# A transformer stack on one core: an eighteenth home for experts' weights, side work placed one unit later, and the first input loaded in smaller pieces

## The chip, the cores and the metric

The kernel runs on one core of one Trainium2 chip. The metric is device time in microseconds (us). Several executions are timed, and their median is compared. TensorE (PE) multiplies, VectorE (DVE) and ScalarE (ACT) do elementwise work, GpSimd (POOL) does little here, and SyncE (SP) issues nearly all DMA transfers.

## What is computed

256 tokens of width 1024 pass through a first block of two layers and then a second block of two layers. Cut to what matters for this change:

```python
def first_block(x, ...):                    # two layers
    for i in range(2):
        mix = (gla_mixer, mlstm_mixer)[i](h, ...)
        h = layer_norm(ALPHA * h + mix, ...)
        ffn = grouped_moe(h, router_w, moe_w1[i], moe_w3[i], moe_w2[i])
        h = layer_norm(ALPHA * h + ffn, ...)

def grouped_moe(t, ...):                    # 16 experts, each token uses 2
    for e in range(16):
        h = silu(t @ w1[e]) * (t @ w3[e])   # 1024 x 512 each
        y = y + gates[:, e] * (h @ w2[e])   # 512 x 1024

def second_block(x, ...):                   # two layers of two attentions and an MLP
    for l in range(2):
        parts = rms(x) modulated @ w_in     # q, k with rms and rotation, v, gates
        x = x + gt1 * ((gate_a * y_a + gate_b * y_b) @ w_out)
        x = x + gt2 * (relu(h2 @ w_ff1) ** 2 @ w_ff2)
```

All operands are float32. All of the weights are read once from HBM, 420 MB in all.

## The kernel before, in words

**Chunks, halves and units.** The weights come as chunks of 128 x 2048 floats, 1 MB each, in the order of use (`build`, L3235). A chunk has two halves, and a half is a unit of PE work. For most products a half is split: ACT copies it rounded into `hi` (L1661) and DVE subtracts into `lo` (L2111), and PE multiplies hi and lo apart. There are five pairs of hi and lo buffers. The experts' chunks are used raw, without a split. Between the weights lie chunks named `ada`, which DVE alone uses: it adds each one, scaled, to a sum (`ada_step`, 2.3 us apiece).

**Homes.** A chunk lies in a home of 8 KB per partition. Six homes `raw0` to `raw5` are always there. While an experts' stage runs, buffers that it doesn't need are homes too: `ACC`, pieces of the big scratch `AR`, and the five `ring` homes, which lie over the hi and lo buffers. `spare` (L3255) lists triples (home, first, last): the home is opened for the chunk `first` of the stage and may be used again up to `last`. `places` (L145) gives each chunk its home: the one opened for it, or the open one used longest ago. An experts' stage has 96 chunks and 17 homes in turn before the change.

**The load queue.** SP goes through the chunks in order (`load`, L2978). Before a transfer it waits until the home's last chunk is used up, and, where a home is opened, for what else used that memory: the ring homes wait for the last unit before the stage (`ring_free`, L750), ACC for `sum_up`, the home `ar2048` in the first stage for `x` (0, 1), which is DVE's last ln_x step. A chunk whose home isn't free holds up all that follow.

**The order of the work.** One generator per stage (`walk_gla` L256, `walk_moe` L303, `walk_mlstm` L390, `walk_attention` L511) yields jobs in one order, and each of the five engines runs through the same generator and does its own share of each job. So a job's place in the generator is its place in the queue of every engine. Between the units of a projection stands side work (`Side.advance`), so many jobs after each unit.

- In an experts' stage `p` counts pairs of experts (0 to 7) and `s` the steps of four units (3.65 us of PE each). A `gather` of PE, DVE and ACT writes the tokens of four experts, in four parts `gather g, 0..3`, into half `g % 2` of XG, which is the buffer `TF` (the same memory as `T2`, whose halves are TH and TL elsewhere). Group 1 is read from p = 2 on; its parts stand at p = 0 (s = 2 and 3) and p = 1 (s = 1 and 4).
- In the mLSTM mixer, `pace` (L450) says how much side work follows each unit of `og`: 0, 1, 2, then 3. `scores 3` follows the second unit, and `values` (0, 0) and (1, 0) the third. On DVE `scores 3` is the weighting of the scores. `values` on PE waits for it.
- In the attentions, `rope n` is a chain of DVE jobs on segment n of q and k (its last is `rope_add`, L2823), and `qk_turn n` (L1491) the transposes of its result on PE, which come LAG = 2 units later (`turns`, L520).

**The start.** The input xT (1 MB, as eight blocks k) comes in two transfers into F with the first half chunk between them, in the order SP L3022 to L3030: x 0, first half, x 1, second half of chunk 0, `vec`, chunk 1, `cst`, chunk 2, `wgu` (34 KB). ACT and DVE split x in four `xs` jobs and the weights in `hi` and `lo`. PE does unit 0, then `glr` (needs all of x, and vec), unit 1, then `z` (needs wgu), and then the next units.

## Time and profile before

| | us |
|---|---|
| three timed runs | 1482.96, 1483.88, 1484.76 |
| median | 1483.88 |
| the profiled execution, its own time | 1485.66 |
| its span in the trace | 1483.8 |
| PE busy | 1443.6 |
| DVE busy | 910.2 |
| ACT busy | 626.7 |
| bytes moved | 420.17 MB |

The profile is of one execution. Its span is 1.9 us shorter than its own time, which holds what lies before the first and after the last instruction. A row of a timeline gives start, duration, engine, line, operation, output and inputs, and in brackets the idle time of the engine just before and what ended it. "issue" there means that the profile shows nothing that the engine waited for. Matmuls overlap, so their durations add up to more than the time between their starts.

### The profile page before, as it was taken

The page shows a single profiled execution, that of the slowest core. Times are in us where ns is not written, and L with a number is a line of the kernel's source. Part 1 is how long each engine was busy: PE and PEld are TensorE (multiplying, and loading weights), DVE is VectorE, ACT ScalarE, POOL GpSimd, SP SyncE. Part 2 cuts the span into 40 slices and gives each one's busy share as a digit, 9 for nine tenths or more (in the row PEclk, how much of TensorE's full clock was granted, in tenths as well). Part 3 has the DMA queues.
Part 4 walks back from the last instruction along what each step waited for, and adds up shares of the span by engine and source line. Part 5 has one row for each costly group of instructions (what it writes and reads, how often), then busy time and mean ns, then how long its engine had stood idle before and what let it go on. Part 6 is the DMA issues. An engine that isn't in the chain of part 4 may idle for free.

```text
span 1483.8 us, 20474 instructions
## 1 busy us (share of the span) xinstructions
PE 1443.6 (97%) x8383; PEld 1068.5 (72%) x8383; DVE 910.2 (61%) x1549; ACT 626.7 (42%) x1004; POOL 40.8 (3%) x39
## 2 busy tenths in 40 slices
PE   9999999989999999999799999999999999999998
PEld 7885444436888544443578897999988898799997
DVE  4986111118787611111799888997968976775555
ACT  6453211115334321211555655454456566465443
POOL 0000000000000000000210000000002000000000
PEclk9999999999999999999899999999999999999999
DMA  9897999998467899999665463899955533445540
GB/s 379 314 365 301 426 427 426 427 426 329 166 247 297 331 424 427 427 426 426 247 231 184 181 232 142 335 369 352 357 182 187 197 123 125 151 170 193 179 168 29
DMA packets 59062, 420.17 MB, mean 283 GB/s; under 512 B 6657, under 2 KB 6721, under 8 KB 8658
## 3 DMA queue, kind: packets, MB, share of 16 engines
q1 hardware_dynamic: 58322, 417.17, 71.5%
q0 software_dynamic: 640, 1.61, 0.4%
q8 instruction: 69, 1.13, 0.3%
q14 instruction: 31, 0.25, 0.0%
HBM read 417.71 MB, written 1.05 MB: 282 GB/s over the span
## 4 chain that ended last, share of the span: by engine, by line
PE 80%; DVE 11%; DMA 4%; ACT 3%; issue 1%; SPq 0%; DVEq 0%; ACTq 0%
PE ps L869 78%; DVE lo L2111 2%; DMA AR<-in_moe 2%; DMA raw<-in_moe 2%; DVE AR L2104 2%; PE ps L1520 1%; DMA AR<-in_wgu 1%; DVE AR L2101 1%; PE ps L1491 1%; ACT AR L2011 1%; PE ps L1244 1%; DVE TINY L2104 1%; DVE ACC L2104 0%; PE ps L991 0%; PE ps L1001 0%
## 5 line engine op out<-in xcount | busy, mean ns | idle before, releaser
L2111 DVE TENSOR_TENSOR lo<-raw,hi 128x1024 fp32r<-128x1024 f32 x296 | 359.4, 1237 | 97.7 <-ACT hi L1661 97.0
L1661 ACT ACTIVATE hi<-raw 128x1024 fp32r<-128x1024 f32 x296 | 306.2, 1056 | 183.3 <-PE ps L869 178.1
L869 PE MATMUL ps<-T,hi 128*128 128x256 f32 x1792 | 323.8, 283 | 1.4 <-DVE lo L2111 0.6
L869 PE MATMUL ps<-hi,T 128*128 128x512 f32 x896 | 285.8, 396 | 1.0 <-DVE lo L2111 0.6
L869 PEld LDWEIGHTS ps<-T,hi 128*128 128x128 f32 x1792 | 277.1, 189 | 10.0 <-issue 5.1
L869 PE MATMUL ps<-T,lo 128*128 128x256 f32 x896 | 249.2, 280 | 0.0
L869 PEld LDWEIGHTS ps<-hi,T 128*128 128x128 f32 x896 | 169.0, 189 | 38.0 <-DVE lo L2111 2.1
L869 PE MATMUL ps<-lo,T 128*128 128x512 f32 x448 | 172.8, 390 | 0.0
L869 PEld LDWEIGHTS ps<-T,lo 128*128 128x128 f32 x896 | 169.2, 189 | 0.3 <-DVE lo L2111 0.3
L869 PE MATMUL ps<-hi,AF 128*128 128x512 f32 x512 | 163.3, 391 | 0.0
L2104 DVE SCALAR_TENSOR_TENSOR AR<-AR,ps 128x512 f32<-128x512 f32 x52 | 35.4, 684 | 192.0 <-PE ps L869 104.8
L869 PE MATMUL ps<-raw,TF 128*64 128x512 f32 x424 | 128.2, 595 | 3.0 <-issue 3.0
L869 PE MATMUL ps<-AR 128*64 128x512 f32 (+7 forms) x612 | 108.6, 408 | 4.7 <-POOL AR L2907 1.3
L869 PEld LDWEIGHTS ps<-hi,AF 128*128 128x128 f32 x512 | 96.2, 188 | 19.5
L869 PE MATMUL ps<-AR,TF 128*64 128x512 f32 x328 | 107.7, 595 | 0.5 <-DMA AR<-in_moe 0.5
L1857 ACT ACTIVATE AF<-ps,TINY 128x512 fp32r<-128x512 f32 x32 | 22.0, 688 | 195.5 <-PE ps L869 195.5
L2104 DVE SCALAR_TENSOR_TENSOR AF<-ps,TINY,AF 128x512 fp32r<-128x512 f32 x32 | 24.0, 750 | 124.6 <-ACT AF L1857 124.6
L869 PE MATMUL ps<-lo,AF 128*128 128x512 f32 x256 | 99.9, 390 | 0.0
L869 PEld LDWEIGHTS ps<-lo,T 128*128 128x128 f32 x448 | 84.5, 189 | 16.8
L869 PEld LDWEIGHTS ps<-raw,TF 128*64 128x64 f32 x424 | 39.5, 137 | 63.2 <-issue 62.4
L869 PEld LDWEIGHTS ps<-AR 128*64 128x64 f32 (+2 forms) x612 | 58.8, 163 | 33.6 <-issue 20.8
L2104 DVE SCALAR_TENSOR_TENSOR ACC<-raw,TINY,ACC 128x2048 f32<-128x2048 f32 x28 | 65.6, 2344 | 0.2
(247 smaller groups left out, 1730.5 us busy)
## 6 DMA issues: line engine op xcount, KB each, us to landing
raw<-in_moe SPq DMA_DIRECT2D x76, 1024.0 KB, 17.1
raw<-in_b_ff SPq DMA_DIRECT2D x64, 1024.0 KB, 5.3
AR<-in_moe SPq DMA_DIRECT2D x59, 1024.0 KB, 17.1
raw<-in_ada SPq DMA_DIRECT2D x48, 1024.0 KB, 6.7
ring<-in_moe SPq DMA_DIRECT2D x45, 1024.0 KB, 15.8
raw<-in_b_in SPq DMA_DIRECT2D x24, 1024.0 KB, 6.0
raw<-in_b_gate SPq DMA_DIRECT2D x16, 1024.0 KB, 4.8
ACC<-in_moe SPq DMA_DIRECT2D x12, 1024.0 KB, 20.2
```

Source lines behind the costliest of these rows:

```text
L869: return e.matmul(o, l, r, start=a, stop=z, skip_group_check=True)
L1244: ins = e.transpose(p[:, 128 * f:128 * f + 128], m.GR[:, 128 * f:128 * f + 128], ident)
L1491: ins = e.transpose(p[:, 256 * x + 128 * q:256 * x + 128 * q + 128], m.RT[n % 2][:, q, 128 * (p0 + x):128 * (p0 + x) + 128], ident)
L1520: ins = e.transpose(p[:, 256 * k + 128 * q:256 * k + 128 * q + 128], m.PB[j % 8][:, q, 128 * k:128 * k + 128], ident)
L1661: e.activation(hi[n % NC][:, :], raw[place[c]][:, 1024 * half:1024 * half + 1024], ACT.Copy).then_inc(*to("hi", "hi", n))
L1857: e.activation(m.YH[:, HALF[n]], PS[bank["down", i, x, n]][:, :], ACT.Copy, scale=m.GS[:, x:x + 1]).then_inc(*to("tile_out", "y_hi", i, x, n))
L2011: ins = e.activation(o, src, ACT.Exp, scale=m.SC, bias=mx[:, q:q + 1], accum_out=sm[:, 2 + 2 * k + q:3 + 2 * k + q])
L2101: return e.tensor_scalar(o, a, s1, s2, op0=op0, op1=op1)
L2104: return e.scalar_tensor_tensor(out=o, in0=a, scalar=s, in1=b, op0=op0, op1=op1)
L2111: tt(lo[n % NC][:, :], r, hi[n % NC][:, :], SUB).then_inc(*to("lo", "lo", n))
```

## The change

It has four parts, in the order in which they act:

1. The input: xT comes in four transfers of 256 KB instead of two of 512 KB, and the first half chunk in two of 256 KB, in the order x 0, w 0, x 1, w 1, x 2, x 3. The split of that half chunk and its products are divided the same way (`hi_first`, `lo_first`, and a job `rest` for the second part), and unit 0 waits piece by piece.
2. The second half of TF becomes home 13, for chunk 11 of each experts' stage alone; it opens with `ring_free`. Ring, ACC and (in the first stage) ar2048 open one, one and two chunks later. That half of TF is XG's group 1, so the four gathers of group 1 move behind chunk 11's use: two at p = 1, s = 2 and two at p = 1, s = 4.
3. In the mLSTM mixer the pace becomes 0, 0, 3, 3, ...: `scores 3` moves behind the third unit of `og` and stands directly before the two `values` there.
4. In both attentions `qk_turn 0` comes one unit later.

```diff
--- before.py
+++ after.py
@@ -256,8 +256,10 @@
 def walk_gla(feed):
     for g in range(4):
         yield ("xs", g)
+        if g == 0:
+            yield from feed.ahead(1)
         if g == 1:
-            yield from feed.ahead(1)
+            yield ("rest",)
 
     def prepare():
         yield [("glr",), ("constants",)]
@@ -359,9 +361,9 @@
         if 0 < p < 8 and s == 4:
             yield ("turn", p)
         if p < 6:
-            for k, at in enumerate((1, 4) if p else (2, 3)):
+            for k, at in enumerate((2, 2, 4, 4) if p == 1 else (1, 4) if p else ()):
                 if s == at:
-                    yield ("gather", p // 2 + 1, 2 * (p % 2) + k)
+                    yield ("gather", p // 2 + 1, k if p == 1 else 2 * (p % 2) + k)
 
     for p in range(9):
         for s in range(6):
@@ -447,7 +449,7 @@
         yield ("turn", 0)
         yield ("turn", 1)
 
-    pace = iter((0, 1, 2) + 13 * (3,))
+    pace = iter((0, 0) + 14 * (3,))
     yield from run_b("og", 2, 8, feed, lambda: side.advance(next(pace)), end=gate_first)
     route = routing()
     rows = iter([[("ln_x", t, s)] for t in range(2) for s in range(2)] + 4 * [[]])
@@ -517,7 +519,7 @@
         yield [("rope_norm", n)]
         for q in range(len(SEGS[n][0])):
             yield [("rope_turn", n, q)]
-        turns.append([LAG, n])
+        turns.append([LAG + (n == 0), n])
         pending.append(n)
         yield [("rope_add", n)]
 
@@ -713,7 +715,7 @@
         chunks, stops = small["chunks"], small["stops"]
         place, before, turn, uses = places(chunks, [s for i in range(2) for s in small["spare"][i]])
         raw += [ACC, ar(4096, 2048), ar(6144, 2048), ar(11264, 2048), ar(13312, 2048), ar(15360, 2048), ar(2048, 2048)]
-        raw += [x[:, :] for x in ring] + [ar(0, 2048)]
+        raw += [x[:, :] for x in ring] + [ar(0, 2048), TF[:, 2048:4096]]
         ACCS = [ACC[:, :], ar(11264, 2048), ar(13312, 2048)]
         plan = Feed(chunks, ())
         while plan.at < len(plan.events):
@@ -723,7 +725,7 @@
         def loaded(c, half=1):
 
             if c == 0 and half == 0:
-                return after("head")
+                return after("head", 1)
             return signal(f"raw{place[c]}"), 16 * turn[c]
 
         def emptied(c):
@@ -902,14 +904,16 @@
                 if u == 0:
 
                     n0 = plan.units[u][2]
-                    w.wait_ge(*after("hi", n0))
                     for ks in (range(4), range(4, 8)):
-                        for k in ks:
-                            if k % 2 == 0:
-                                w.wait_ge(*after(*xs[k // 2]))
-                            mm(o, hi[n0][:, 128 * k:128 * k + 128], th[:, k, :], k == 0, False)
-                            mm(o, hi[n0][:, 128 * k:128 * k + 128], tl[:, k, :], False, False)
-                        w.wait_ge(*after("lo", n0))
+                        w.wait_ge(*after("hi", n0) if ks[0] else after("hi_first"))
+                        for k in (ks[0], ks[2]):
+                            w.wait_ge(*after("xs_hi", k // 2))
+                            for j in (k, k + 1):
+                                mm(o, hi[n0][:, 128 * j:128 * j + 128], th[:, j, :], j == 0, False)
+                            w.wait_ge(*after(*xs[k // 2]))
+                            for j in (k, k + 1):
+                                mm(o, hi[n0][:, 128 * j:128 * j + 128], tl[:, j, :], False, False)
+                        w.wait_ge(*after("lo", n0) if ks[0] else after("lo_first"))
                         for k in ks:
                             ins = mm(o, lo[n0][:, 128 * k:128 * k + 128], th[:, k, :], False, k == kt - 1)
                 else:
@@ -1077,8 +1081,8 @@
                     elif what == "glr":
                         p = take("glr")
                         glr = VE["glr"].rearrange("p (k r) -> p k r", k=8)
-                        w.wait_ge(*after("x_t", 0))
-                        w.wait_ge(*after("x_t", 1))
+                        for g in range(4):
+                            w.wait_ge(*after("x_t", g))
                         w.wait_ge(*after("vec"))
                         for k in range(8):
                             ins = mm(p[0:16, 0:256], glr[:, k, :], F[:, k, :], k == 0, k == 7)
@@ -1651,6 +1655,10 @@
 
                 u = plan.splits[n]
                 c, half, _ = plan.units[u]
+                if n == 0:
+                    w.wait_ge(*after("head", 0))
+                    e.activation(hi[0][:, HALF[0]], raw[place[c]][:, HALF[0]], ACT.Copy).then_inc(*to("hi", "hi_first"))
+                    return
                 w.wait_ge(*loaded(c, half))
                 if n >= NC:
                     w.wait_ge(*after("used", plan.splits[n - NC]))
@@ -1722,8 +1730,11 @@
                         hi_part(a[0])
                     elif what == "xs":
                         two = slice(2 * a[0], 2 * a[0] + 2)
-                        w.wait_ge(*after("x_t", a[0] // 2))
+                        w.wait_ge(*after("x_t", a[0]))
                         e.activation(TH[:, two, :], F[:, two, :], ACT.Copy).then_inc(*to("column", "xs_hi", a[0]))
+                    elif what == "rest":
+                        w.wait_ge(*loaded(0, 0))
+                        e.activation(hi[0][:, HALF[1]], raw[place[0]][:, HALF[1]], ACT.Copy).then_inc(*to("hi", "hi", 0))
                     elif what == "glr":
                         w.wait_ge(*after("glr"))
                         w.wait_ge(*after("gl_one"))
@@ -2106,6 +2117,10 @@
             def lo_part(n):
 
                 c, half, _ = plan.units[plan.splits[n]]
+                if n == 0:
+                    w.wait_ge(*after("hi_first"))
+                    tt(lo[0][:, HALF[0]], raw[place[c]][:, HALF[0]], hi[0][:, HALF[0]], SUB).then_inc(*to("lo", "lo_first"))
+                    return
                 w.wait_ge(*after("hi", n))
                 r = raw[place[c]][:, 1024 * half:1024 * half + 1024]
                 tt(lo[n % NC][:, :], r, hi[n % NC][:, :], SUB).then_inc(*to("lo", "lo", n))
@@ -2331,6 +2346,9 @@
                         two = slice(2 * a[0], 2 * a[0] + 2)
                         w.wait_ge(*after("xs_hi", a[0]))
                         tt(TL[:, two, :], F[:, two, :], TH[:, two, :], SUB).then_inc(*to("v_split", "xs", a[0]))
+                    elif what == "rest":
+                        w.wait_ge(*after("hi", 0))
+                        tt(lo[0][:, HALF[1]], raw[place[0]][:, HALF[1]], hi[0][:, HALF[1]], SUB).then_inc(*to("lo", "lo", 0))
                     elif what == "constants":
                         u, g0 = tiny("c_u", 8), small["vec"][0]["gla_g"][0]
                         w.wait_ge(*after("c_tanh"))
@@ -2971,7 +2989,7 @@
 
         def sync_program(e):
             w = Waits(e)
-            xT = D["xT"].rearrange("p (g k i) -> p g k i", g=2, k=4)
+            xT = D["xT"].rearrange("p (g k i) -> p g k i", g=4, k=2)
             opens = {first: (i, p) for i in range(2) for p, first, _ in small["spare"][i]}
             first_of = {c0 - 12: i for c0, i in stops.items()}
 
@@ -2985,7 +3003,7 @@
                     i, q = opens[c]
                     if q == 0:
                         w.wait_ge(*after("sum_up", (0, i)))
-                    elif 6 < q < 12:
+                    elif 6 < q < 12 or q == 13:
                         w.wait_ge(*after(*ring_free(i)))
                     elif i == 0:
                         if q > 5:
@@ -3019,9 +3037,10 @@
                     at["f_load", i, x] = (signal(f"full_raw{i}"), 96 * (x + 1))
                 v.wait_ge(*after("f_done", i))
 
-            e.dma_start(F[:, 0:4, :], xT[:, 0]).then_inc(*landed("x_t", 0))
-            e.dma_start(raw[0][:, 0:1024], chunks[0][1][:, 0:1024]).then_inc(*landed("head"))
-            e.dma_start(F[:, 4:8, :], xT[:, 1]).then_inc(*landed("x_t", 1))
+            for g in range(4):
+                e.dma_start(F[:, 2 * g:2 * g + 2, :], xT[:, g]).then_inc(*landed("x_t", g))
+                if g < 2:
+                    e.dma_start(raw[0][:, HALF[g]], chunks[0][1][:, HALF[g]]).then_inc(*landed("head", g))
             load(0, 1024)
             e.dma_start(vec[:, :], D["vec"]).then_inc(*landed("vec"))
             load(1)
@@ -3249,10 +3268,10 @@
             i, at = int(n[3]), len(chunks) - count
             moe[i] = chunks[at:]
             stops[len(chunks)] = i
-            early = (((4, 0, 95), (5, 1, 76), (3, 5, 5), (1, 6, 95), (2, 7, 95), (6, 19, 95)) if i == 0 else
+            early = (((4, 0, 95), (5, 1, 76), (3, 5, 5), (1, 6, 95), (2, 7, 95), (6, 21, 95)) if i == 0 else
                      ((12, -2, 95), (6, -1, 95), (1, 5, 95), (2, 7, 95), (5, 10, 76)))
-            ring = tuple((7 + n, 11 + n, 80) for n in range(5))
-            spare[i] = [(p, at + c, at + last) for p, c, last in (*early, *ring, (0, 16, 95))]
+            ring = ((13, 11, 11), *((7 + n, 12 + n, 80) for n in range(5)))
+            spare[i] = [(p, at + c, at + last) for p, c, last in (*early, *ring, (0, 17, 95))]
     small = {"cst": (cst_at, D["cst"].shape[1]), "vec": (vec_at, D["vec"].shape[1]), "chunks": chunks, "stops": stops, "moe": moe,
              "moe_at": [c - len(moe[i]) for c, i in stops.items()], "spare": spare}
     return two_block_kernel(nc, aps, out, small)
```

## Rows read from the trace of the kernel before

**Rows 1.** The page's part 4: share of the chain that ended last, by engine.
```profile
PE 80%; DVE 11%; DMA 4%; ACT 3%; issue 1%; SPq 0%; DVEq 0%; ACTq 0%
```

**Rows 2.** Windows in the two experts' stages: busy us of each engine, PEclk, DMA share, GB/s.
```profile
134.00:136.00 2.00, 2.00 (x18) 1.42 (x14) 0.34 (x1) 0.00 (x0) 0.00 (x0) 1.00 0.48 147
141.00:144.00 3.00, 2.38 (x12) 0.73 (x9) 2.79 (x13) 0.00 (x0) 0.00 (x0) 1.00 0.58 167
508.00:511.00 3.00, 3.00 (x20) 1.90 (x20) 1.52 (x3) 0.00 (x0) 0.00 (x0) 1.00 0.72 213
250.00:300.00 50.00, 50.00 (x242) 19.99 (x240) 6.38 (x12) 7.74 (x14) 0.00 (x0) 1.00 1.01 426
```

**Rows 3.** Timeline of PE, end of the first experts' stage.
```profile
304.68 3.65 PE L869 MATMUL ps<-AR,TF 128*64 128x512 f32 x16 [0.47 <-DMA AR<-in_moe]
...
319.71 0.61 PE L869 MATMUL ps<-AR 128*64 128x512 f32 x1 [0.48 <-DMA raw<-in_moe]
...
324.57 3.65 PE L869 MATMUL ps<-raw,AR 128*64 128x512 f32 x16 [0.61 <-DMA raw<-in_moe]
329.39 0.61 PE L869 MATMUL ps<-ACC,AR 128*64 128x512 f32 x1 [1.17 <-issue]
```

**Rows 4.** Timeline of SP's queue, start of the first experts' stage.
```profile
118.16 2.28 SPq L3005 DMA_DIRECT2D ring<-in_moe  x5
...
134.52 7.28 SPq L3005 DMA_DIRECT2D AR<-in_moe  x3
```

**Rows 5.** Timeline of PE at p = 0, s = 2 of the first experts' stage.
```profile
143.70 0.39 PE L869 MATMUL ps<-FR,AF 128*128 128x256 f32 x1 [0.62 <-DVE FR L2455]
```

**Rows 6.** Timeline of PE, end of the second experts' stage.
```profile
696.69 3.65 PE L869 MATMUL ps<-AR 128*64 128x512 f32 x16 [0.43 <-DMA AR<-in_moe]
...
701.52 0.61 PE L869 MATMUL ps<-ACC,AR 128*64 128x512 f32 x1 [1.18 <-issue]
```

**Rows 7.** Timeline of PE and DVE in the mLSTM mixer's `og`.
```profile
440.47 3.49 DVE L2111 TENSOR_TENSOR lo<-raw,hi 128x1024 fp32r<-128x1024 f32 x3
440.69 1.55 PE L869 MATMUL ps<-AR 128*128 128x256 f32 x8 [1.29 <-DVE AR L2104]
...
443.87 0.55 DVE L2104 SCALAR_TENSOR_TENSOR AR<-ps,AR 128x384 f32<-128x384 f32 x1
...
444.34 2.34 DVE L2104 SCALAR_TENSOR_TENSOR ACC<-raw,TINY,ACC 128x2048 f32<-128x2048 f32 x1
...
444.85 0.50 PE L869 MATMUL ps<-cst,AR 128*128 128x1 f32 x4
...
446.60 2.35 DVE L2111 TENSOR_TENSOR lo<-raw,hi 128x1024 fp32r<-128x1024 f32 x2
```

**Rows 8.** Timeline of PE and DVE in the first attention: `qk_turn 0`, `rope_add 1`, `qk_turn 1`.
```profile
756.89 1.97 PE L1491 MATMUL ps<-cst,AR 128*128 128x128 f32 x8 [2.65 <-DVE AR L2823]
...
767.29 0.96 DVE L2823 TENSOR_TENSOR AR<-AR 128x768 f32<-128x768 f32 x1
...
770.14 0.82 PE L1491 MATMUL ps<-cst,AR 128*128 128x128 f32 x6
```

**Rows 9.** Timeline of PE and DVE in the second attention, the same three.
```profile
1136.34 1.10 PE L1491 MATMUL ps<-cst,AR 128*128 128x128 f32 x8 [1.08 <-DVE AR L2823]
...
1146.73 0.96 DVE L2823 TENSOR_TENSOR AR<-AR 128x768 f32<-128x768 f32 x1
...
1148.20 0.82 PE L1491 MATMUL ps<-cst,AR 128*128 128x128 f32 x6
```

**Rows 10.** Window after the wait of Rows 8, columns as in Rows 2.
```profile
756.00:760.00 4.00, 3.11 (x12) 2.87 (x13) 3.97 (x4) 1.20 (x2) 0.00 (x0) 0.57 0.24 47
```

**Rows 11.** Timeline of PE at the start: `glr` and `z`.
```profile
11.09 3.63 PE L869 MATMUL ps<-F,vec 128*16 128x256 f32 x16
...
18.30 1.95 PE L869 MATMUL ps<-AR 17*128 17x512 f32 x4 [0.51 <-DMA AR<-in_wgu]
```

**Rows 12.** DMA issues: tensors, queue, count, KB each, median us from issue to landing.
```profile
F<-in_xT SPq DMA_DIRECT2D x2, 512.0 KB, 5.3
out_dram<-X SPq DMA_DIRECT2D x4, 256.0 KB, 2.0
```

## The prediction

> **What bounds the kernel now.** I read the chain that ended last first: PE holds 80% of it, DMA 4%, DVE 11% [rows 1]. So a change pays only where PE stands still, and I looked for those places with PE's timeline, and for their cause with windows and with SP's queue. In the experts' stages the DMA runs at 426 GB/s with a share of 1.01 while PE is busy too [rows 2]; PE uses chunks faster than they come, lives on what the homes held at its start, and runs dry near the end: 0.47 + 0.48 + 0.61 + 1.17 = 2.73 us in the first stage [rows 3] and 0.43 + 1.18 = 1.61 us in the second [rows 6]. The two waits marked "issue" stand before the step that reads ACC, in the run of DMA waits, so I count them as DMA. Elsewhere PE waits for DVE: 1.29 us in og [rows 7], 2.65 and 1.08 us at `qk_turn 0` [rows 8, 9].
>
> Of the profiled execution's 1485.66 us, 1483.8 are span; it lies 1.78 us above the median of 1483.88. I sum against it and take the difference over to the median. About 0.2% (3.0 us) is what a measurement of this kernel can tell from no change.
>
> **The experts' stages (part 2).** In a stage that the DMA ends, only idle time of the DMA after it has begun can be won. The five ring loads are issued at 118.16, the next ones that wait for PE at 134.52, three of them over 7.28 us [rows 4]. In between and after, the DMA falls to 147 GB/s for 2 us and to 167 GB/s for 3 us [rows 2]. Against 426 GB/s that is 2 x 279/426 = 1.31 and 3 x 259/426 = 1.82, together 3.13 us. The extra chunk takes 1.05 MB / 426 GB/s = 2.46 us and is issued with the ring, so it covers the first gap and pushes the rest of the queue back. The second gap is the third load of 134.52, which waited for DVE's last ln_x (the home ar2048) and held the loads behind it; it now stands two chunks later, behind a load whose home is free at about the end of s = 1. I take both gaps as closed: -3.13 us. PE can use that much: its DMA waits are 2.73 us, and 0.62 us of waiting for `one_hot 1` goes as the gather moves away [rows 5], in all 3.35. **First stage: -3.1 us.** In the second stage there is one gap, 213 GB/s over 3 us [rows 2], 3 x 213/426 = 1.50 us, and the waits of 1.61 can take it. **Second stage: -1.5 us.** Bounds for the pair: 0 (the idle time only moves) and -3.35 - 2.23 = -5.6, all of PE's waits with 0.62 in each. The gathers are the same count; they move from p = 0 to p = 1 and end at the same s = 4, a step before p = 2 reads them, and PE has the slack of the waits at the end. SP issues no more transfers here, only another address.
>
> **The mLSTM pace (part 3).** The wait of 1.29 us before `scores 3` goes: the third unit starts at 440.69 - 1.29 = 439.40, and the unit and the scores, which took 444.85 - 440.69 = 4.16 us [rows 7], are done at 443.56. But now the job's place on DVE has moved too. Between the old place and the new one DVE's order holds an ada step and a lo. Before, DVE did three lo, the weighting (443.87), ada (444.34), lo (446.60) [rows 7], and was never idle. After, it does three lo until 443.87, ada for 446.60 - 444.34 = 2.26, lo for 2.35 / 2 = 1.18 and only then the weighting, 0.55: done at 447.86. `values` (0, 0) needs it and now stands right behind the scores, so PE starts it at about 447.9 where it started at 444.85: **+3.05 us**, a wait of 4.3 us in place of one of 1.29. The units and values after it shift as a whole; the next lo are early enough.
>
> Such a wait has a second price. After the wait of 2.65 us [rows 8] the granted clock was 0.57 of full over the next 4 us, that is mostly at 1.2 instead of 2.4 GHz [rows 10], and the same jobs from `qk_turn 0` to `qk_turn 1` took 770.14 - 756.89 = 13.25 us there and 1148.20 - 1136.34 = 11.86 us behind the wait of 1.08 [rows 8, 9]. I charge that 1.39 once: **+1.4**. Part 3: +4.45; bounds -1.3 (no new wait) and +5.85 (two such stretches).
>
> **`qk_turn 0` a unit later (part 4).** In the first attention PE is free at 756.89 - 2.65 = 754.24. It does a unit first, and the result of `rope_add 0` is then there. The wait goes, and so does the slow stretch: after 11.86 us of the same jobs PE stands at `qk_turn 1` at 766.10. `rope_add 1` ends at 767.29 + 0.96 = 768.25, in a chain in which DVE has no gap, so it won't come sooner: a new wait of 2.15 us. `qk_turn 1` starts at 768.3 for 770.14: **-1.84**. Whether 2.15 us of waiting lowers the clock lies between the wait of 1.08 [rows 9], behind which the same jobs ran faster, and that of 2.65; half of 1.39: **+0.7**. Second attention: at `qk_turn 1` by 1136.34 - 1.08 + 11.86 = 1147.12, `rope_add 1` done at 1147.69, start 1147.75 for 1148.20: **-0.45**. Behind that, DVE's next waits are on PE and shift along. Bounds: -4.04 - 1.08 = -5.1 (no new wait) and 0.
>
> **The input (part 1).** Smaller pieces let unit 0 begin and end sooner, by an estimated 1 us (half of 512 KB at 426 GB/s is 0.6 us, and the copies behind it are half as long). Then `glr`, which started at 11.09 without a wait, can come forward, but `z` waits 0.51 us for wgu at 18.30 already [rows 11], and wgu stands behind the same bytes in the same queue. What is won ahead of it becomes a longer wait there, some 1.5 us: **0**. SP issues three transfers more, 2.28 / 5 = 0.46 us each [rows 4], so wgu's issue comes 1.4 us later; the bytes queued ahead of wgu hide that, and without them it would cost those 1.4. Bounds: -0.5 (the wait that is there) and +4.2 (below).
>
> The Trainium skill speaks against this part: DMA: Bandwidth & Descriptors, section Measured (HBM→SBUF, 128 partitions, SWDGE, issued from GpSimd), asks for transfers of at least 1 MiB, and its fit, 2.0 us plus the bytes over 436 GB/s for each, would put three transfers more at 6 us if they ran one after another, an estimate from that page; the sum would then be +4.3 in place of -1.7.
>
> **Sum.** -3.1 - 1.5 + 3.05 + 1.4 - 1.84 + 0.7 - 0.45 + 0 = -1.74: 1485.66 becomes 1483.9, and the median of 1483.88 becomes **1482.1 us**, within what counts as no change, on its fast side.
>
> **Rivals.** (a) *The weighting doesn't end up late.* If DVE comes to it before the ada step's end, or the shift is made up behind it (PE waits again before the heads' transposes, so the chain there isn't all PE), part 3 gives between -1.3 and 0: 1476.4 to 1477.7, taken as 1477. For it: the new wait is worked out from DVE's order alone, and no row shows it. Against: DVE works without a break through that stretch [rows 7]. Chance 0.25, always faster.
> (b) *The extra home does nothing.* The idle time of the DMA moves to a later place, because some other home is late in its turn, and the end of the stage stays: -4.6 goes, 1486.7. Against: in the middle of the stage the DMA has a share of 1.01 [rows 2]. It decides if the DMA's share falls anywhere between the ring loads and the stage's end. Chance 0.10, half of it beyond 0.2% on the slow side.
> (c) *The small transfers pay one by one*, the rival on the slower side. A transfer of 256 KB took 2.0 us alone [rows 12], where its bytes at 426 GB/s need 0.62: 1.4 us more for each. Three more in a row ahead of wgu are +4.2, and a wait at `z` of that length brings the 1.4 of the clock: 1482.1 + 5.6 = 1487.7. It decides from the point where the pieces no longer overlap; against it, a piece of 512 KB lands 5.3 us after its issue [rows 12] while the next ones were issued within 0.5 us, so they overlap now. Chance 0.07. The rule of the page above is this rival.
> (d) *The granted clock takes more*: a second slow stretch in og and one in the first attention, +2.1: 1484.2, still no change; it is held by the forecast's range.
>
> **How the numbers follow.** Forecast with (d): 0.55, own range 1479 to 1485; 0.15 of it lies under 1480.9 and 0.03 above 1486.9. (a) 0.25, (b) 0.10, (c) 0.07, 0.03 for what I don't see. Faster: 0.15 + 0.25 = 0.40. Slower: 0.03 + 0.05 + 0.07 = 0.15. Same: 0.45. The range takes in most of (a) and half of (b): 1475.8 to 1487.0.
>
> **What would show it.** Right: no window under 400 GB/s from the ring loads to the end of either experts' stage, PE's DMA waits there under 1 us; PE waiting some 4 us for a DVE L2104 ahead of `values` with the granted clock under 1 behind it; no wait at `qk_turn 0` and about 2 us at `qk_turn 1` of the first attention; `z` still starting at about 18.3. Wrong: `z` much earlier or later, a PE without a wait in og, or gaps of the DMA in a new place.

## The result and the profile after

The changed kernel took **1488.38 us** (median of 9 runs, 1486.43 to 1489.34) beside 1484.76 us for the kernel before on the same chip (9 runs, 1482.96 to 1486.76). The ratio is 1.0021, with a 95% interval from 1.0012 to 1.0029: slower by 3.6 us, just over what a measurement of this kernel can tell. The forecast was 1482.1 us and no change, with a range up to 1487.0: wrong, in the sign too. Four executions, three of the kernel before and one of a run below, took 2330 us and more; they are left out of every ratio.

The profiled execution of the changed kernel took 1486.71 us at a mean granted clock of 0.994; the nine runs have 0.992 in the mean. (1 - clock) times the span is about the time given up to the clock: 8.9 us in the profiled execution and 11.2 in the mean. So the profile shows the change with 2.3 us less of the slow clock than it usually has.

Windows of the kernel after, columns as in [rows 2]:

```profile
134.00:136.00 2.00, 2.00 (x14) 1.09 (x10) 0.00 (x0) 0.00 (x0) 0.00 (x0) 1.00 1.05 434
141.00:144.00 3.00, 3.00 (x18) 1.00 (x16) 2.79 (x12) 0.00 (x0) 0.00 (x0) 1.00 1.02 431
144.00:146.00 2.00, 2.00 (x12) 0.71 (x10) 0.89 (x2) 0.00 (x0) 0.00 (x0) 1.00 0.97 365
508.00:511.00 3.00, 3.00 (x22) 1.99 (x22) 1.00 (x2) 1.78 (x4) 0.00 (x0) 1.00 1.03 431
446.00:450.00 4.00, 3.65 (x16) 3.32 (x16) 1.34 (x2) 0.00 (x0) 0.00 (x0) 0.61 1.01 426
450.00:454.00 4.00, 4.00 (x12) 3.25 (x12) 0.00 (x0) 0.00 (x0) 0.00 (x0) 0.54 1.02 432
```

The gaps of the DMA of [rows 2] are closed (434 for 147, 431 for 167 and 213 GB/s; 365 in one window is all that is left of them). The last two rows are new: in og PE works at a granted clock of 0.61 and 0.54, that is mostly at 1.2 GHz instead of 2.4, for 6.8 us.

Timeline of the kernel after, PE and DVE, at the places of [rows 3, 7, 8, 11]; the row at 458.73 is where DVE takes over from PE's last `values`, and the one at 469.31 the first step of PE behind the norm of the mLSTM mixer:

```profile
11.56 3.63 PE L871 MATMUL ps<-F,vec 128*16 128x256 f32 x16
18.91 1.95 PE L871 MATMUL ps<-AR 17*128 17x512 f32 x4 [0.66 <-DMA AR<-in_wgu]
...
322.84 3.65 PE L871 MATMUL ps<-raw,AR 128*64 128x512 f32 x16 [0.38 <-DMA raw<-in_moe]
327.68 0.61 PE L871 MATMUL ps<-ACC,AR 128*64 128x512 f32 x1 [1.19 <-issue]
...
442.26 2.35 DVE L2115 SCALAR_TENSOR_TENSOR ACC<-raw,TINY,ACC 128x2048 f32<-128x2048 f32 x1
444.52 1.22 DVE L2126 TENSOR_TENSOR lo<-raw,hi 128x1024 fp32r<-128x1024 f32 x1
445.65 0.55 DVE L2115 SCALAR_TENSOR_TENSOR AR<-ps,AR 128x384 f32<-128x384 f32 x1
446.35 0.58 PE L871 MATMUL ps<-cst,AR 128*128 128x1 f32 x4 [4.54 <-DVE AR L2115]
...
458.73 0.17 DVE L2678 COPY TINY<-ps 128x8 f32<-128x8 f32 x1 [11.39 <-PE ps L871]
...
469.31 1.06 PE L995 MATMUL ps<-cst,AR 128*128 128x128 f32 x8 [0.57 <-DVE AR L2115]
...
761.09 1.09 PE L1495 MATMUL ps<-cst,AR 128*128 128x128 f32 x8
772.50 0.87 PE L1495 MATMUL ps<-cst,AR 128*128 128x128 f32 x6 [2.13 <-DVE AR L2841]
```

The same two rows in the kernel before:

```profile
453.84 0.17 DVE L2660 COPY TINY<-ps 128x8 f32<-128x8 f32 x1 [4.89 <-PE ps L869]
464.42 1.06 PE L991 MATMUL ps<-cst,AR 128*128 128x128 f32 x8 [0.57 <-DVE AR L2104]
```

Read as differences to the rows before, these give the balance of the profile. `z` is 0.61 later (18.30). The two steps with a wait at the end of the first experts' stage come 1.73 and 1.71 earlier (324.57 and 329.39). The step behind the mixer's norm is 4.89 later, so the mixer lost 6.60. From the start of `values` to that point it takes 12.38 us for 8.99 (458.73 - 446.35, 453.84 - 444.85), and from there through DVE and ACT to the step behind the norm 10.58 us in both. `qk_turn 1` of the first attention is 2.36 later (770.14), so 2.53 came back in the second experts' stage and the attention. The span ends 1.1 later.

The kernel's other lines hardly moved: PE holds 80% of the chain that ended last and DVE 12%, for 80% and 11% in [rows 1].

### The profile page after: what moved, and what is told of

The parts are those of the page before. It is cut to its first block, busy times and chain, and to the rows that moved or that the text cites. A ratio compares the mean times of both kernels' runs of the same rounds, so it can differ in the third digit from the quotient of the medians.

```text
span 1484.9 us, 20479 instructions
## 1 busy us (share of the span) xinstructions
PE 1443.7 (97%) x8383; PEld 1068.7 (72%) x8383; DVE 911.3 (61%) x1550; ACT 626.1 (42%) x1005; POOL 39.3 (3%) x39
## 3 DMA queue, kind: packets, MB, share of 16 engines
q8 instruction: 69, 1.13, 0.3%
HBM read 417.71 MB, written 1.05 MB: 282 GB/s over the span
## 4 chain that ended last, share of the span: by engine, by line
PE 80%; DVE 12%; DMA 4%; ACT 3%; issue 1%; SPq 0%; DVEq 0%; ACTq 0%
PE ps L871 77%; DVE lo L2126 3%; DVE AR L2115 2%; DMA AR<-in_moe 1%; DMA raw<-in_moe 1%; PE ps L1524 1%; DMA AR<-in_wgu 1%; DVE ACC L2115 1%; DVE AR L2112 1%; DVE TINY L2115 1%; PE ps L1248 1%; ACT AR L2022 1%; PE ps L995 0%; PE ps L1495 0%; DVE TINY L2112 0%
## 5 line engine op out<-in xcount | busy, mean ns | idle before, releaser
L871 PE MATMUL ps<-raw,TF 128*64 128x512 f32 x432 | 135.0, 595 | 1.4 <-issue 1.4
L871 PE MATMUL ps<-AR 128*64 128x512 f32 (+7 forms) x636 | 126.2, 421 | 3.2 <-POOL AR L2925 1.3
L871 PEld LDWEIGHTS ps<-AR 128*64 128x64 f32 (+2 forms) x636 | 64.9, 165 | 38.5 <-issue 26.7
```

The costliest lines, as they stand in the source:

```text
L871: return e.matmul(o, l, r, start=a, stop=z, skip_group_check=True)
```

## The experiments

All were timed in turns with the kernel before (median 1484.6 to 1485.3 us in the four groups); differences are those of the medians, each to the kernel before of its own group.

**The parts taken apart.** First the change without part 3:

```diff
-    pace = iter((0, 0) + 14 * (3,))
+    pace = iter((0, 1, 2) + 13 * (3,))
```

> The changed kernel with the pace of og put back to 0, 1, 2, 3, ... (parts 1, 2 and 4 stay). Theory A (the weighting late on DVE costs its wait of 3.2 us and then two stretches of PE at half clock, together 6.5 us from og to the next norm, and nothing gives it back): 1488.4 - 6.5 = 1481.9, that is 2.9 under the kernel before; no granted clock under 1 in og. Theory B (the prediction's size, one slow stretch, 4.45 us): 1483.9. Theory C (what DVE loses in og is made up behind it, and the slower time comes from elsewhere): over 1486.5.

Measured: 1481.59 us, ratio 0.9972 (0.9960 to 0.9984), 3.75 less than before; no granted clock under 1 in og. Theory A. Part 3 alone turns a gain into the loss: 1488.4 - 1481.6 = 6.8 us by the medians, 3.6 + 3.75 = 7.4 when each is set against the kernel before that was timed beside it.

The change without part 1 (its hunks of the diff undone):

> The changed kernel with the input loaded as before (parts 2, 3 and 4 stay). Theory A (the split input makes z 0.61 us later, since wgu is issued 2.2 us later, and all that follows shifts by it, the opening of the ring homes too): 0.6 us less, 1487.8, z at 18.3. Theory B (the experts' stage that follows is ended by the DMA and swallows the 0.6): 1488.4, with z at 18.3 all the same. Theory C (the four small transfers help and z was late by chance): over 1488.6.

Measured: 1488.23 us, ratio 1.0018 (1.0010 to 1.0027) where the change has 1.0021; `z` at 18.80 in its profile, where A and B had 18.3. The intervals overlap: this run can't tell A from B. Only that part 1 is not the cause follows.

The kernel before with part 2 alone:

> The kernel before with the eighteenth home alone (part 2: the home, the gathers, the shifted openings). Theory A (the DMA's gap goes, but the last chunks land out of step, as read in the trace of the changed kernel, so PE gets 2.3 us of the first stage and 0.7 of the second): 3.0 less than before. Theory B (the prediction's size, 3.1 and 1.5): 4.6 less. Theory C (the home does nothing by itself, the gain came from other parts): under 1 less.

Measured: 1481.54 us, ratio 0.9974 (0.9965 to 0.9982), **3.8 less**, between A and B. In its profile the last ACT step of the first stage comes 2.13 sooner (338.71 to 336.58), and from there to the end of the second stage another 0.77 (372.14 to 371.37 us): 2.9 of the 3.8, as theory A has it. The rest has no place in the trace; the runs of the two kernels spread by 5 us each.

The kernel before with part 3 alone:

```diff
-    pace = iter((0, 1, 2) + 13 * (3,))
+    pace = iter((0, 0) + 14 * (3,))
```

> The kernel before with the pace 0, 0, 3, 3, ... alone (part 3). Theory A: 6.5 us more than before, with a wait of about 4.4 us ahead of values (0, 0) and two stretches of PE at half clock behind it. Theory B (the prediction's size): 4.45 more, one stretch. Theory C (only in the changed kernel, where the stage starts at another time, is the wait there): under 1.5 more.

Measured: 1493.13 us, ratio 1.0054 (1.0041 to 1.0067), **7.8 more**, over both. Windows of this run behind the wait, columns as before, and its two steps of PE:

```profile
444.00:448.00 4.00, 0.14 (x2) 0.00 (x0) 4.00 (x4) 0.00 (x0) 0.00 (x0) 1.00 0.65 244
448.00:452.00 4.00, 3.32 (x13) 2.99 (x13) 1.67 (x3) 0.00 (x0) 0.00 (x0) 0.60 1.01 424
452.00:456.00 4.00, 4.00 (x13) 3.37 (x14) 0.00 (x0) 0.00 (x0) 0.00 (x0) 0.50 1.01 426
456.00:460.00 4.00, 4.00 (x13) 3.17 (x12) 0.00 (x0) 0.60 (x1) 0.00 (x0) 0.62 1.02 430
```

```profile
448.68 0.89 PE L869 MATMUL ps<-cst,AR 128*128 128x1 f32 x4 [4.54 <-DVE AR L2104]
...
473.25 1.06 PE L991 MATMUL ps<-cst,AR 128*128 128x128 f32 x8 [0.58 <-DVE AR L2104]
```

The wait is the same 4.54 us to the hundredth. What differs is the clock: 10.2 us at half here (0.60, 0.50 and 0.62 in the rows), 6.8 in the changed kernel's profile. The change without part 1 has the same wait of 4.54 us too, and 10.2 us at half, of which 1.6 lie in the wait itself; its two steps are 23.85 us apart (446.23 and 470.08).

**What part 3 costs, in two terms.** To tell the late weighting from the clock, PE was given products of constants to do in the wait. They go into the bank that `values` is about to overwrite, so nothing else changes:

```diff
                         p = take("values1", t, hp)
+                        if t == hp == 0:
+                            for _ in range(10):
+                                mm(p[:, 0:256], C["tri3"][:, 0:128], C["tri3"][:, 0:256], True, True)
```

A first try had 17 products and misjudged their price:

> The kernel before with the pace 0, 0, 3, 3, ... (as in the run that took 7.8 us more), and 17 matmuls of constants on PE (128x256, 0.245 us each by the rows of values, 4.2 us in all) in the wait ahead of values (0, 0); their result is overwritten. The weighting on DVE is as late as before, so the wait itself stays paid. Theory A (of the 7.8 us the late weighting is 3.1 to 3.7, the rest the half clock behind the idle stretch): the granted clock stays 1.00 in og and the time is 3.1 to 3.7 more than before. Theory B (the clock has no part; the late values hold up DVE's chain to the next norm by more than their own delay): still 7 to 8 more, whatever the clock. Theory C (the clock falls for the kind of work behind, not for the idle stretch): clock 0.5 behind the fill all the same, and 7 to 8 more.

Measured: 1491.66 us, 7.1 more than before. Each product shows as two matmuls in the trace, and the fill took 7.50 us instead of 4.2, so `values` itself came 2.6 us later still (it starts 111.90 us behind the last ACT step of the experts' stage, for 109.28 in the run before this and 106.14 in the kernel before). The clock stayed at 1.00. Undecided, but the price was now known, and 10 products fit:

> Part 3 alone with 10 products of constants in the wait ahead of values (0, 0), 0.44 us each as the first fill showed, 4.4 us for a wait of 4.5. Theory A (the loss of 7.8 is 3.1 of late weighting and 4.7 of half clock behind the idle stretch): values (0, 0) starts 3.1 to 3.3 later than in the kernel before, og's norm by the same, granted clock 1.00, time 3.0 to 4.0 more than before. Theory B (the loss lies behind the late values and not in the clock): 7 to 8 more.

Measured: 1488.18 us, ratio 1.0020 (1.0011 to 1.0028), **3.0 more**. Timeline and windows of this run:

```profile
443.12 4.48 PE L869 MATMUL ps<-cst 128*128 128x256 f32 x20
447.12 0.55 DVE L2107 SCALAR_TENSOR_TENSOR AR<-ps,AR 128x384 f32<-128x384 f32 x1
447.73 0.61 PE L869 MATMUL ps<-cst,AR 128*128 128x1 f32 x4
...
467.38 1.06 PE L991 MATMUL ps<-cst,AR 128*128 128x128 f32 x8 [0.56 <-DVE AR L2107]
```

```profile
443.00:447.00 4.00, 4.00 (x21) 3.54 (x20) 4.00 (x3) 0.07 (x1) 0.00 (x0) 1.00 0.64 217
447.00:451.00 4.00, 3.87 (x24) 3.25 (x23) 1.81 (x3) 0.00 (x0) 0.00 (x0) 1.00 1.02 426
```

The weighting is as late as before and `values` waits for it as long, but PE isn't idle, and the clock stays at 1.00. Theory A: of the 7.8 us 3.0 are the late weighting and 4.8 the clock, the one good to 1.3 us and the other to about 2 by the intervals. The clocks of the runs agree: in the mean they are 0.9916 with the idle wait and 0.9951 with the filled one, as in the kernel before beside it (0.9951); 0.0035 of the span is 5.2 us. The Trainium skill says it in TensorE: Matmul & The Clock Gate, section Part 1: The HAM clock gate (the "warmup" mystery): "the default state is throttled, and activity releases the throttle". This trace agrees, with 0.50 behind 4.54 us of idling and 1.00 behind the same time filled.

**Where units can't cover.** If `values` only lacks the weighting, a unit of PE ahead of it should hide the wait. Two paces on parts 2 and 4 (which alone run at 3.6 under before, below):

```diff
-    pace = iter((0, 1, 2) + 13 * (3,))
+    pace = iter((0, 0, 1, 2) + 12 * (3,))   # the second run: (0, 0, 1, 0) + 12 * (3,)
```

> Parts 2 and 4 with the pace 0, 0, 1, 2, 3, ...: scores 3 behind the third unit as in the change, but the two values behind the fourth. Theory A (PE runs in order, so what the weighting lacks is covered by one unit of 2.85): the wait ahead of values is 4.5 - 2.85 = 1.7 in place of 4.5, the wait of 1.29 is gone, the clock stays up after so short a wait: +0.4 against parts 2 and 4 with the old pace, no change that can be measured. Theory B (any wait over 1.5 there lowers the clock): +2 to +4. Theory C (the late weighting was not the cause of the loss, but scores 3 behind the third unit): +6.5.

> Parts 2 and 4 with the pace 0, 0, 1, 0, 3, ...: scores 3 behind the third unit, values behind the fifth, so that two units of 2.85 stand between them. Theory A (the only harm was the wait for the weighting): no wait of PE for the weighting at all, -1.3 against parts 2 and 4 with the old pace. Theory B (the later values make the norm behind og late, which is then waited for): 0 to +2. Theory C (scores 3 behind the third unit is the harm): +6.5.

Measured: 1488.72 us (ratio 1.0019, 1.0008 to 1.0030) and 1485.81 us (1.0011, 1.0002 to 1.0020), that is 7.0 and 4.1 more than parts 2 and 4. My theory A fell in both. By size none holds: the first run fits C's 6.5, but the second contradicts C, and both passed B. In kind it is B, as the profiles show. Timeline of PE, the steps `values` (0, 0) and the one behind the norm, first run and second:

```profile
445.17 0.58 PE L869 MATMUL ps<-cst,AR 128*128 128x1 f32 x4 [1.78 <-DVE AR L2104]
...
468.10 1.94 PE L991 MATMUL ps<-cst,AR 128*128 128x128 f32 x8 [3.29 <-DVE AR L2104]
```

```profile
446.43 0.50 PE L869 MATMUL ps<-cst,AR 128*128 128x1 f32 x4
...
465.96 1.94 PE L991 MATMUL ps<-cst,AR 128*128 128x128 f32 x8 [6.04 <-DVE AR L2104]
```

In the second run nothing waits for the weighting any more, and yet PE stands still for 6.04 us, at the norm. Take the distance between the two steps in every run: 464.42 - 444.85 = 19.57 us before, 19.65 with the fitting fill, 19.53 here; 22.96 and 22.93 where 6.8 us of half clock lie in it, 24.57 with 10.2. It has two parts. The four `values` and the one unit of PE between them, which every pace here leaves there, take 9.0 us at full clock until DVE takes over, and 12.4 to 14.0 where part of them is at half; then the norm on DVE and ACT takes 10.6 us in all these runs. The units of PE behind `values` are the cover of the norm, and a unit moved ahead of `values` is a unit less behind it. So at full clock the start of `values` sets the end, and each pace that puts it off loses that much: 2.53 and 3.79 us in these two (445.17 and 446.43 for 442.64 with parts 2 and 4). The rest is the clock: in the first run 6.8 us at half follow the wait of 1.78 and another 6.8 go with the wait of 3.29 at the norm, in the second 6.8 go with the wait of 6.04.

**Part 4.** The kernel before with parts 2 and 4:

> The kernel before with parts 2 and 4 (home and qk_turn 0 a unit later; input and pace as before). It stands beside the run of the home alone (3.8 less than before) and the run without the pace (3.75 less). Theory A (part 4 wins what the trace of the changed kernel shows, 1.75 and 0.35, and the input costs 0.6): 5.5 less than before. Theory B (part 4 gives its gain back, since PE's wait only moves to qk_turn 1 and lowers the clock there in many runs, and the input costs nothing): 3.8 less. Between: 4.5 less if only one of the two holds.

Measured: 1481.72 us, ratio 0.9972 (0.9963 to 0.9981): **3.6 less**, theory B; part 2 alone had 3.8. The two intervals leave room for some 2 us either way, so the times don't exclude the forecast's -1.6 for part 4; the steps say more. Why nothing is left of the 1.8 that the profiles of before and after differ by shows in the profile of part 2 alone, where PE also waits 2.65 us at `qk_turn 0`, but the clock stays up. The two turns there, and with parts 2 and 4:

```profile
753.64 1.09 PE L1491 MATMUL ps<-cst,AR 128*128 128x128 f32 x8 [2.65 <-DVE AR L2823]
765.52 0.81 PE L1491 MATMUL ps<-cst,AR 128*128 128x128 f32 x6
```

```profile
753.94 1.09 PE L1491 MATMUL ps<-cst,AR 128*128 128x128 f32 x8
765.36 0.87 PE L1491 MATMUL ps<-cst,AR 128*128 128x128 f32 x6 [2.10 <-DVE AR L2823]
```

From the end of the experts' stage (707.95 and 707.89) `qk_turn 1` is at 57.57 and 57.47: the same. One wait has taken the place of another, 2.10 for 2.65, and the turn comes 0.1 us sooner at equal clocks. The 1.8 compared a turn behind a stretch of half clock [rows 8, 10] with one that has none behind its wait.

Does that wait's clock cost anything? Products of constants were put into the wait at `qk_turn 1`, as in `values` above. A first try with 8 took 3.62 us for a wait of 2.10:

> Parts 2 and 4 (3.6 less than before), with 8 matmuls of constants on PE in the wait of 2.13 us that part 4 leaves at qk_turn 1 of the first attention; their result is overwritten. Theory A (part 4's gain of 1.75 was given back to a stretch of PE at half clock behind that wait in most runs): clock 1.00 behind it and 1.0 to 1.8 less than parts 2 and 4 alone, so 4.6 to 5.4 less than before. Theory B (the clock behind that wait doesn't matter, part 4 gains nothing because DVE's chain sets the end): the same as parts 2 and 4, 3.6 less than before.

It gave 1480.63 us, 4.0 less than before, between the theories, with a fill 1.5 us longer than the wait. With 4 products:

> Parts 2 and 4 with 4 products (1.8 us) in the wait of 2.13 at qk_turn 1 of the first attention. Theory A (part 4's gain goes to the half clock behind that wait): no wait over 0.5 there, no slow stretch behind it, 5.0 to 5.6 less than before (parts 2 and 4 alone: 3.6 less). Theory B (DVE's chain of the rotation sets the end of the stage, so that part 4 has nothing to win): 3.6 to 4.0 less.

Measured: 1478.94 us, ratio 0.9957 (0.9944 to 0.9970), **6.3 less**: theory A. Windows of PE behind the turn, without the fill, then with it:

```profile
767.00:771.00 4.00, 4.00 (x13) 3.18 (x12) 3.73 (x13) 0.34 (x1) 0.00 (x0) 0.63 0.74 262
```

```profile
767.00:771.00 4.00, 4.00 (x19) 3.32 (x18) 3.73 (x13) 1.15 (x2) 0.00 (x0) 1.00 0.73 262
```

PE does 19 matmuls in place of 13 in the same 4 us, and the last turn of the stage comes 1.68 sooner (93.98 and 92.30 us behind the experts' end). The times differ by 2.7, with intervals that overlap. The clocks of all executions bear it out: 0.993 to 0.995 in the eleven without the fill, 0.995 to 0.998 in the five with it, 0.9945 and 0.9964 in the mean, and the difference is 2.8 us of the span. Of that the stretch behind the turn is 1.7 us (3.4 at half); the rest of it falls elsewhere. The better cure is to have no wait: a unit more for the first two turns, then for all.

```diff
-        turns.append([LAG + (n == 0), n])
+        turns.append([LAG + (n < 2), n])        # the second run: LAG + 1 for every n
```

> Parts 2 and 4, with qk_turn 1 a unit later as well (LAG + 1 for n under 2). Theory A (the wait of 2.13 that part 4 left at qk_turn 1 goes and nothing takes its place; no slow stretch behind it): 2 to 3 less than parts 2 and 4. Theory B (DVE's chain of the rotation is the bound; the wait moves on to qk_turn 2): within 0.7 of parts 2 and 4.

> Parts 2 and 4 with every qk_turn a unit later (the run with the first two a unit later came out 6.0 under before, with a wait of 1.09 left at the fourth turn). Theory A (units of PE cover what DVE's chain lacks): no wait at any turn of the first attention, 0.5 to 1.1 less than with two, 6.5 to 7 under before. Theory B (the last turn is what the scores wait for, so a later one only moves the wait behind it): 6.0 under before or less.

Measured: 1479.33 us (ratio 0.9966, 0.9952 to 0.9979) and **1478.32 us** (0.9948, 0.9935 to 0.9961), 6.0 and 6.9 less than before. Theory A in both by size. In the first a wait of 1.09 us is left at the fourth turn; in the second PE waits for no turn of the first attention, and 0.4 us is the sum of its waits from 735 to 830 us. Parts 2 and 4 with every turn a unit later beat the kernel before and the changed one. The two runs' intervals overlap, so the step from the one to the other isn't shown by the times.

**Part 1.** Alone:

> The kernel before with the input part alone (part 1). Theory A (wgu issued later makes z 0.6 later, and nothing behind gives it back): z at about 18.95 where the profiled runs with the old input have 17.96 to 18.85, mean 18.4; 0.6 more than before. Theory B (the start is at most as late as in other runs): z at 18.4, 0.0 more. Theory C (the prediction's rival, small transfers paid one by one): z at 22, 4 to 5 more.

Measured: 1485.50 us, ratio 1.0008 (0.9999 to 1.0016), 0.9 more, `z` at 19.06. In the 13 profiles with the old input `z` starts at 17.96 to 18.85, mean 18.42; in the three with the split input and the full fill at 18.91 to 19.14, mean 19.04. So the start is 0.6 later (A); the time doesn't exclude zero. There is a second price that I had not foreseen. Windows of this run behind `z`:

```profile
20.00:22.00 2.00, 2.00 (x8) 1.22 (x7) 1.47 (x4) 2.00 (x5) 0.00 (x0) 0.75 1.02 430
22.00:24.00 2.00, 2.00 (x11) 2.00 (x11) 1.22 (x1) 1.98 (x3) 0.00 (x0) 0.50 0.98 397
```

PE is at half clock for 3.4 us, which costs 1.7. So it is in three of the five profiles with the split input, and in none of the 13 with the old one. What brings it on isn't shown: the waits at `z` are 0.55, 0.67 and 1.04 us in the three, 0.66 and 1.05 in the two without. With wgu's transfer ahead of the second half of chunk 0:

> The input part alone with wgu's transfer issued right behind the input's, ahead of the second half of chunk 0, vec, chunk 1 and cst. Theory A (z waits for wgu, because wgu is issued late and stands behind their bytes): no wait of PE for wgu, z at 17.9 to 18.4, 0.5 to 1.0 less than the input part alone. Theory B (z is late because PE itself comes later, wgu is only just behind): z within 0.2 of the input part alone, the wait for wgu gone and another ahead of it.

Measured: 1486.17 us (ratio 1.0010, 1.0002 to 1.0019), 1.6 more than before, `z` at 19.47. It waits 0.67 us for ACT, as it did 0.55 in the input part alone; in the changed kernel it was wgu (0.66). It comes 0.4 later and not within 0.2, as `glr` now waits 0.75 us for vec; but theory A is out, and B's reason holds without its size. The late issue of wgu, which I had taken for the cause, isn't it. Last, the split input with a shorter fill at the start:

```diff
-                for _ in range(8):
+                for _ in range(5):
                     mm(p[0:64, 0:256], ...
```

> The split input alone with five products in place of eight in the fill that PE runs from 1.33 us on (it ends by 5.3 instead of 7.5; its result is never used). Theory A (PE's fill kept unit 0 from starting when the first pieces were there): unit 0 starts at 5.8 in place of 7.49, but glr needs the last piece and comes at 11.5 as before: z at 18.9 to 19.1, no change to the split input with the full fill. Theory B (unit 0 and with it glr come forward by 1 us or more): z at 18.0 or sooner, 0.5 to 1 less than the split input with the full fill. Theory C (the shorter fill leaves PE idle long enough to lower the clock in unit 0): z at 19.5 or later, 1 to 2 more.

Measured: 1486.67 us (ratio 1.0006, 0.9997 to 1.0015), 1.5 more than before by the medians. Timeline of PE in this run:

```profile
1.34 3.80 PE L871 MATMUL ps<-AR 128*64 128x256 f32 x10 [1.34 <-POOL AR L2925]
5.71 1.34 PE L871 MATMUL ps<-T,hi 128*128 128x256 f32 x6 [0.57 <-ACT hi L1660]
10.96 3.63 PE L871 MATMUL ps<-F,vec 128*16 128x256 f32 x16
18.70 1.95 PE L871 MATMUL ps<-AR 17*128 17x512 f32 x4 [1.04 <-DMA AR<-in_wgu]
```

Theory A, nearly: unit 0 starts at 5.71 instead of 7.49, `glr` gains 0.6 on the changed kernel and `z` 0.3 on the mean of 19.04, and the time shows nothing. What the pieces cost I read in the DMA's packets from 2 to 9 us, before and after:

```profile
DMA packets 655, 2.29 MB, mean 327 GB/s; under 512 B 65, under 2 KB 65, under 8 KB 652
```

```profile
DMA packets 962, 1.96 MB, mean 280 GB/s; under 512 B 103, under 2 KB 103, under 8 KB 962
```

Pieces of half the size have packets of half the length, and 2.04 KB a packet in the mean carry less in the same time than 3.50 KB: 0.33 MB less by 9 us, 0.8 us of the DMA at 426 GB/s, though its queues are busy 90% of that time, for 93% before. ACT's copies of the chunks behind come 0.9 later (17.37 for 16.47), and `glr`'s copy and `z` stand behind them. That the packets are the reason is read from these two profiles; no run tried it apart.

## Why the prediction was wrong

**The step that failed** is the second price of part 3, "I charge that 1.39 once: **+1.4**", a term of the right kind and the wrong size. Behind the wait the clock stayed at half for 6.8 to 10.2 us and cost 3.4 us in the changed kernel's profile (22.96 - 19.57), 4.3 without part 1 (23.85 - 19.57), 5.0 with part 3 alone (24.57 - 19.57), 4.8 by the runs with and without the fill. I took the price from the one slow stretch that I had in sight, of 3.4 us behind a shorter wait of 2.65 us [rows 10]; even my upper bound of two such stretches, +5.85 for the part, was passed by the measured 6.8 to 7.8. With 4.8 for 1.4 alone the sum would have been 1.7 above before instead of 1.7 below. The other parts erred the same way by less: against their own runs part 2 was short by 0.8 us, part 1 by 0.9 and part 4 by 1.8, each uncertain by more than 1.

**What held of part 3.** The weighting behind the ada step and a lo, the wait in place of the one of 1.29, its size (4.54 us for 4.3) and the shift of `values` (+3.17 for +3.05; 3.0 by the filled run). Rival (a) fell: nothing behind made the shift up, because behind `values` lie 9.0 us of PE and 10.6 of DVE and ACT, and nothing in them gave way in any run. That the shift goes through as a whole I had said without that reason.

**Part 2.** The gaps were found and closed as forecast, but of 4.6 us the profiles show 3.0 (after: 1.67 + 0.61 = 2.28 in the first stage, 0.71 in the second) and the times 3.8. In the first stage the DMA has moved 1.13 MB more by 316 us, 2.7 us of its time, but the last steps of PE that wait for a chunk come only 1.72 sooner. The assumption that what the DMA gains PE gains too was too simple; in what order those bytes landed wasn't tried. The waits of 0.38 and 1.19 at the end also break my test of under 1 us: a stage that the DMA ends still ends in waits. The last two steps stand 4.84 us apart (327.68 - 322.84; 4.82 before) and the first takes 3.65, so as long as the DMA ends the stage, the wait of 1.17, which I had counted among those that could go, stays. Rival (b) fell.

**Part 4.** By the rows it came as forecast: no wait at `qk_turn 0`, one of 2.13 at `qk_turn 1` (2.15), 1.80 less from the experts' end to that turn (1.84). But "the wait goes, and so does the slow stretch" took the clock of one profile for the kernel's. At equal clocks the turn comes 0.1 sooner, and the times show no gain, with room for 2 us either way.

**Part 1.** "**0**", since the bytes ahead of wgu would hide its later issue, was wrong by 0.6 at `z`: the later issue doesn't count, but the bytes themselves come later; and by a half clock behind `z` in three profiles of five. Rival (c) had the right sign and five to seven times the size: 0.6 to 0.9 us for three transfers more, 0.2 to 0.3 each, where it had 1.4. The rule of the Trainium skill, DMA: Bandwidth & Descriptors, section Measured (HBM→SBUF, 128 partitions, SWDGE, issued from GpSimd), points the right way. The fit stands in that page's section Anatomy of one DMA — SWDGE (gpsimd) path; its 6 us, an estimate for pieces one after another, isn't what this case shows, where `z` is 0.6 later.

Rival (d), the clock taking more, was the true one: I had put it inside the forecast with +2.1 and no chance of its own. Put together by the runs of single parts, the ratios less one are +0.0008, -0.0026, +0.0054 and -0.0002 (part 4 as the difference of two runs), in all +0.0034, for +0.0021 measured; each has an interval of about 0.001 to either side.

## What to carry to other kernels

Ask of every wait that a change makes what the engine does meanwhile: an idle PE can pay twice, once for the wait and once for the slow clock behind it, and in og the second was the larger; products of constants in the wait saved 4.8 us in og, and a unit moved into it cured the turns without them. But where a chain of another engine follows the step, a unit moved ahead of it is taken from that chain's cover: measure the chain first, and if its length is the same whatever stands beside it, the start of the step is what counts. Split a first transfer only if the consumer of the *last* piece gains.

## What the hardware showed that I had not expected

How long the clock stays low depends on the run and not only on the wait. With the same 4.54 us there were 6.8 us at half in one profile and 10.2 in two others, though PE was busy from the wait's end on. Behind 2.1 us there was a slow stretch with parts 2 and 4 alone and none in the changed kernel's profile (772.50); behind 2.65 us one before [rows 10] and none with the home alone; behind 1.78 us in og there was one. Behind 1.29 us in og there was none in any profile, and yet the wait of 1.35 us at some 1107 us, ahead of the second attention, had 3.4 us at half with it in 8 of the 18 profiles, the kernel before among them:

```profile
1107.00:1111.00 4.00, 3.90 (x19) 3.70 (x20) 3.44 (x10) 3.65 (x8) 0.00 (x0) 0.62 0.02 9
```

A wait of 6.65 us ahead of the first attention is in every profile, and 6.8 to 13.7 us at half go with it. So the length of a wait didn't tell its price here, and a profile's clock behind a wait is one draw: a gain that rests on it has to be checked on a profile without it.

A product of constants with 128 x 256 outputs in float32 shows as two matmuls and takes 0.44 us at full clock, 0.22 for each row counted, and I had read the rows of `values` as one product each.
